# Gate stage of a hybrid decoder step: GpSimd takes key pages 0 and 2, VectorE 1 and 3, the sums run in another order, and the state's store is issued one piece sooner

## The reference, cut to what matters

```python
# attend_sample: q (8, 1, 8 heads, 2, 64), k_past (8, 512, 8, 2, 64) through the page table
s_past = einsum('bqhcd,bkhcd->bhcqk', q, k_past) * scale
p = softmax(s)[:, :, 0] - lam * softmax(s)[:, :, 1]
o = einsum('bhqk,bkhv->bqhv', p, v_past) + (the new token's own share)
# hgrn_steps, one step per sample
S = exp(g) * S + k * v
o = q . S
```

## Time and profile before

| what | us |
|---|---|
| median of 3 runs | 2257.0 |
| the three runs | 2255.3, 2257.0, 2257.14 |
| the profiled execution, its own time | 2256.59 |
| its span in the trace | 2254.8 |
| what lies around the span | 1.8 |
| gate stage on PE, first to last piece | 1092.7 to 1271.7 |
| PE busy over the span | 2221.8 (99%) |
| DVE, ACT, POOL busy over the span | 1542.2 (68%), 1140.3 (51%), 957.7 (42%) |

### The profile page before, as it was taken

How to read it: one execution, slowest core, us unless ns; L and a number is a source line. 1 busy time by engine, 2 the same in 40 slices (tenths; PEclk the granted TensorE clock), 3 DMA queues, 4 the chain that set the end, 5 groups by cost and what they waited for, 6 DMA issues and landing times. The chain is left out here.

```text
span 2254.8 us, 47757 instructions
## 1 busy us (share of the span) xinstructions
PE 2221.8 (99%) x18881; PEld 2104.7 (93%) x18881; DVE 1542.2 (68%) x2534; ACT 1140.3 (51%) x2343; POOL 957.7 (42%) x1149
## 2 busy tenths in 40 slices
PE   7999999999999999999999999999999999999999
PEld 5899998989999999989888899999999999999999
DVE  4668677777767687776678515417988888876535
ACT  6666665666666666665433402015466666643110
POOL 1135262634444352635444314442155666535431
PEclk9999999999999999999999999999999999999999
DMA  8212122231213121221699713111355554485212
GB/s 308 85 54 90 48 86 67 58 105 55 99 48 105 42 81 60 67 95 39 237 363 353 272 41 123 48 48 62 129 188 188 184 191 180 181 310 194 88 47 95
DMA packets 103513, 288.34 MB, mean 128 GB/s; under 512 B 18426, under 2 KB 26490, under 8 KB 103290
## 3 DMA queue, kind: packets, MB, share of 16 engines
q1 hardware_dynamic: 102138, 281.09, 35.7%
q10 hardware_dynamic: 1152, 4.19, 0.5%
HBM read 213.18 MB, written 63.77 MB: 123 GB/s over the span
## 5 line engine op out<-in xcount | busy, mean ns | idle before, releaser
L172 PE MATMUL h_G<-xn_hi,h_w_hi 128*128 128x344 f32 x1368 | 457.8, 335 | 0.2 <-ACT h_d_oraw L920 0.2
L172 PE MATMUL h_G<-xn_hi,h_w_lo 128*128 128x344 f32 x1368 | 437.3, 320 | 0.0
L172 PE MATMUL h_G<-xn_lo,h_w_hi 128*128 128x344 f32 x1368 | 437.0, 319 | 0.0
L1205 POOL TENSOR_TENSOR h_w_lo<-h_w_raw,h_w_hi 128x1024 fp32r<-128x1024 f32 x58 | 149.3, 2574 | 385.5 <-ACT h_w_hi L782 349.8
L172 PEld LDWEIGHTS h_G<-xn_hi,h_w_hi 128*128 128x128 f32 x1368 | 258.6, 189 | 32.6 <-issue 21.2
L172 PEld LDWEIGHTS h_G<-xn_lo,h_w_hi 128*128 128x128 f32 x1368 | 257.3, 188 | 4.6
L172 PEld LDWEIGHTS h_G<-xn_hi,h_w_lo 128*128 128x128 f32 x1368 | 257.3, 188 | 0.0
L3094 DVE SCALAR_TENSOR_TENSOR x<-t_ps,keep_mod,x 128x344 f32<-128x344 f32 x168 | 94.2, 570 | 161.9 <-PE t_ps L2931 99.5
L2931 PE MATMUL t_ps<-f_act_lo,f_d_hi 128*128 128x344 f32 x528 | 169.5, 321 | 0.0
L2931 PE MATMUL t_ps<-f_act_hi,f_d_lo 128*128 128x344 f32 x528 | 168.9, 320 | 0.0
L2931 PE MATMUL t_ps<-f_act_hi,f_d_hi 128*128 128x344 f32 x528 | 168.4, 319 | 0.0
(11 more groups left out here) (471 smaller groups left out, 6997.1 us busy)
## 6 DMA issues: line engine op xcount, KB each, us to landing
h_w_raw<-in_w_in SPq DMA_DIRECT2D x72, 512.0 KB, 3.7
y_rows<-f_y SPq DMA_DIRECT2D x44, 516.0 KB, 2.7
f_y_pair<-y_rows SPq DMA_DIRECT2D x22, 1032.0 KB, 5.2
h_d_ada_w<-in_w_ada SPq DMA_DIRECT2D x32, 512.0 KB, 4.2
g_kp<-in_cache_k SPq DMA_DIRECT2D x32, 512.0 KB, 6.3
g_vp<-in_cache_v SPq DMA_DIRECT2D x32, 512.0 KB, 5.8
f_a<-in_w_ffn SPq DMA_DIRECT2D x57, 256.0 KB, 2.7
h_w_raw<-in_w_mix SPq DMA_DIRECT2D x24, 512.0 KB, 3.6
```

The costliest lines, as they stand in the source:

```text
L172: ins = eng.matmul(out, w[:, k * P:(k + 1) * P], x[:, k, columns], start=(k == 0 and n == 0), stop=(k == n_k - 1 and n == 2))
L1205: pool.tensor_tensor(wlo[w][:, :], raw[r][:, :], whi[w][:, :].bitcast(F32), ALU.subtract).then_inc(lo_done.sem, 1)
```

## The change

GpSimd multiplies pages 0 and 2 in place of 2 and 3, VectorE 1 and 3 in place of 0 and 1. VectorE sums the pages in the order 1, 0, 3, 2, and SP's and POOL's waits count by that order: the load of the next sample's page j still waits for the sum of page j. ACT issues the state's store ahead of the evacuation of piece `TURN_AT[i] + 1`, one piece sooner; the `finish_tile` that went with the last store stays where it was. No operation is added or removed.

```diff
+SUM_ORDER = (1, 0, 3, 2)
+POOL_KEYS = (0, 2)
@@ sync
-                    sp.wait_ge(k_summed.sem, k_summed.at(i, j + 1))
+                    sp.wait_ge(k_summed.sem, k_summed.at(i, SUM_ORDER.index(j) + 1))
@@ scalar
-                if n - 2 in TURN_AT:
-                    i = TURN_AT.index(n - 2)
+                if n - 1 in TURN_AT:
+                    i = TURN_AT.index(n - 1)
                     act.wait_ge(st_new.sem, st_new.at(i, 1))
                     act.dma_start(flat(o["s_state"][bass.ds(i, 1)]), st[:, :]).then_inc(st_out.sem, 16)
-                    if i == NS - 1:
-                        for t in cut_tiles(i):
-                            finish_tile(t)
+                if n - 2 == TURN_AT[NS - 1]:
+                    for t in cut_tiles(NS - 1):
+                        finish_tile(t)
@@ gpsimd
-                for j in (2, 3):
+                for j in POOL_KEYS:
@@ vector
-                for j in range(PAGES):
-                    if j < 2:
+                for j in SUM_ORDER:
+                    if j not in POOL_KEYS:
...
-                        dve.wait_ge(k_scaled.sem, k_scaled.at(i, j - 1))
+                        dve.wait_ge(k_scaled.sem, k_scaled.at(i, POOL_KEYS.index(j) + 1))
```

## The result

| kernel | median, us | runs | lowest to highest |
|---|---|---|---|
| before | 2256.52 | 6 | 2255.30 to 2258.20 |
| changed | 2266.50 | 6 | 2263.12 to 2269.64 |

The changed kernel is slower: the ratio is 1.0043 (95% interval 1.0033 to 1.0053), 10.0 us in the medians. The profiled execution took 2268.26 us (span 2266.5), 11.7 more than the profiled one of before.

The account below looks back on a forecast made before the run. PE, busy 99% of the span, was taken as the bound; -0.3 + 0.75 + 2.4 + 2.8 - 0.9 - 0.4 + 0.5 = +4.9 us gave 2261.9 us, range 2253.5 to 2267.

Parts of the forecast that it names:

- the store's landing: Gate stage: store taken to land in 7.5 us, bounds 3.7 or no gain; first key page 19.7 us behind store issue.
- the steps for turns 0 to 6: Gate stage, between successive samples' score transposes: +0.75 first, +2.4 for the next three, then +2.8, -0.9 and -0.4 us.
- The lock: Gate stage: such DVE operations and POOL multiplications exclude each other for whole instructions; whichever asked first goes first.
- `low` behind POOL's pages: Gate stage: in some turns `low` asks ahead of DVE's page 3, costing between 0 and 2.4 us; +0.5 taken.
- turn 5: Sample 5's gate turn: next page 0 lands 9.7 us after its score transposes start, behind both cuts; -0.9 us.
- the rival in which the store lands fast: Gate stage: store needs 3.7 us, POOL's passes fall among the state update's multiplications; 2265.4 us, chance 0.15.
- Turn 4: Sample 4's gate turn: POOL's page 0 holds line 1972, PE waits 2.5 us for the state; 23.6 us long, +2.8.
- Turn 6: Sample 6's gate turn: the next page 0 comes behind `cut`, keys end at 17.9 where before 18.3; -0.4 us.
- T7: Start of sample 7's score transposes: PE still waits over 2 us there, clock loss kept, everything behind moves along.
- turn 0's own keys: Sample 0's keys at the gate stage's start: between 0 and 0.65 us of PE's wait goes; -0.3 taken.
- the store at the end of the state update: Gate stage: the store goes out when the new state is ready, 7.8 us after the score transposes start.
- nothing lost in ACT's queue: Gate stage: the store moves past one evacuation, one issue is 0.34 us; taken to cost nothing.

Follow-up runs that it names:

- pool_behind_cut: The changed kernel, with POOL's key multiplications held until DVE's `cut` of the turn is done: 2259.03 us, ratio 1.0010.
- order_only: The changed kernel's page order and shares, with the state's store back at its old place: 2264.23 us, ratio 1.0033.
- pool_memset: The changed kernel with each POOL key multiplication replaced by three memsets of the page, products of pages 0 and 2 left out: 2252.51 us, ratio 0.9980.

## Why the prediction was right, and where its sizes were off

The sign and the mechanism were right, and the time lay in the range, near its upper end. The sum was half of what came: +4.9 against +10.0. That the time still fell into the range is owed to the range's width, which was drawn for the bounds of the store's landing. In the sum itself a slip is without weight: 20.0 + 20.6 + 20.0 less 58.1 is 2.5 and not 2.4, which would make the total 4.95 in place of 4.85. With the last experiments each half can be weighed: POOL's pages ahead of DVE are worth 7.5 us (pool_behind_cut) where the steps for turns 0 to 6 sum to 4.65, and `low` is worth 4.2 where the step had 0.5. The two take away 11.7 one at a time and 12.1 together.

*The lock, and who goes next: right but for one row.* Turn 0 of the changed kernel, DVE, then POOL, beside the earlier trace rows:

```profile
1115.61 2.86 DVE L1895 TENSOR_SCALAR gate_a<-gate_a 128x1032 f32<-128x1032 f32 x1
1118.39 3.40 DVE L1905 TENSOR_TENSOR g_kp<-g_kp,gate_b 128x1024 f32<-128x1024 f32 x1
1121.83 2.34 DVE L1909 TENSOR_REDUCE g_s_tok<-g_kp 128x16 f32<-128x1024 f32 x2
1124.09 3.37 DVE L1905 TENSOR_TENSOR g_kp<-g_kp,gate_b 128x1024 f32<-128x1024 f32 x1
...
1115.51 5.20 POOL L1874 TENSOR_TENSOR g_kp<-g_kp,gate_b 128x1024 f32<-128x1024 f32 x2 [5.72 <-DMA g_kp<-in_cache_k]
1123.99 2.39 POOL L1868 TENSOR_TENSOR h_w_lo<-h_w_raw,h_w_hi 128x1024 fp32r<-128x1024 f32 x1 [3.28 <-ACT h_w_hi L1702]
```

POOL asks for page 0 at T + 7.7 (1115.51), 0.1 us ahead of `cut`, which waits and takes 2.86; DVE's page 1 ends at 1121.79, T + 14.0. Both are to the tenth what was forecast. Turn 1 (19.75 for 20.0) and turn 2 (20.4 for 20.6) came within 0.3, though turn 2 by another course, below.

*`low` behind POOL's pages: mis-sized.* The next row of DVE is where it fails. Page 3's multiplication is asked for at 1124.09, `low` at 1123.99, so it takes 3.37 in place of 1.2: 2.1 us in turn 0, which the step knew as a bound for all turns together and gave 0.5. The bound was that of one pass; the same happens in turn 3 too, there to page 1. In turn 6 of this kernel `low` came behind page 1 and was itself held; only in pool_behind_cut does it hold page 3 there. Before, both of DVE's multiplications stood at the head of the turn and only sums, which nothing held, were left by the time `low` came. In the order 1, 0, 3, 2 a multiplication stands late in the turn, and it meets `low`.

*The store's landing: mis-sized, with turns 2, 3, 5 and 6.* The step took 7.5 us, "since the same loads stand ahead of it". Stores 1 to 4 landed in 4.7, 4.5, 5.6 and 5.2, while stores 5 and 6 needed 8.3 and 8.1. SP's key loads and next state load, which follows the landing, and ACT's store of sample 1; first of the changed kernel, then of pool_behind_cut:

```profile
1128.79 3.66 SPq L1621 DMA_DIRECT2D g_kp<-in_cache_k  x4
1142.36 0.33 SPq L1624 DMA_DIRECT2D g_st<-in_state  x1
...
1137.62 0.34 ACTq L1741 DMA_DIRECT2D out_s_state<-g_st  x1
```

```profile
1128.75 3.66 SPq L1621 DMA_DIRECT2D g_kp<-in_cache_k  x4
1141.70 0.33 SPq L1624 DMA_DIRECT2D g_st<-in_state  x1
...
1134.59 0.34 ACTq L1741 DMA_DIRECT2D out_s_state<-g_st  x1
```

The key loads go out at the same time in both. The store goes 3.0 us later in the changed kernel, since its turn 0 was longer, and is down only 0.7 later: 9.9 us behind the end of the key loads' issue (1128.79 + 3.66) against 9.3. Stores 2 to 4, issued 3.8 to 4.5 later than in pool_behind_cut by the same measure, are down 1.3 to 1.8 later. So the loads ahead weigh more in the landing than the store's own issue, and in a stretched turn they have drained further. In order_only a store as late as T + 15.5 landed in 5.0. The key pages therefore came sooner against the stretched turns: from store to POOL's start on the next-but-one sample's page 0 it took 16.7 us in turn 2, 16.3 in turn 3 and 17.2 in turn 5, where the step had 19.7; 20.3 in turn 6. In turn 5 POOL began at T + 7.1, where 9.7 was forecast, and held both cuts (2.69 and 2.88). So the rival in which the store lands fast came half true: POOL's passes fell among the state update in turns 2 and 3, turns 5 and 6 took 21.1 and 19.9 where it gave 20.6 and 20.0 and the sum 19.2 and 17.9, and its 2265.4 is nearer to the result than the forecast. But no store landed in its 3.7 us, and those of turns 5 and 6 needed over 8. Of the page DMA: Bandwidth & Descriptors of the Trainium skill ("Queues, rings and completion order") it was said that by its rule of taking queues in turn the store would not stand behind SP's loads. The rows on store 1 lean against that, without settling it. That the draining is the cause is read from the rows of these kernels, not isolated by a run of its own.

What the sooner pages do, POOL above DVE, in turn 2 and turn 3:

```profile
1154.33 7.52 POOL L1874 TENSOR_TENSOR g_kp<-g_kp,gate_b 128x1024 f32<-128x1024 f32 x2 [1.02 <-DMA g_kp<-in_cache_k]
...
1153.93 1.20 DVE L1966 TENSOR_TENSOR g_st<-g_st,keep_s_f 128x1024 f32<-128x1024 f32 x1
1155.07 1.21 DVE L1972 TENSOR_TENSOR g_vB<-g_vB,keep_s_kk 128x1024 f32<-128x1024 f32 x1
1156.31 3.32 DVE L1974 TENSOR_TENSOR g_st<-g_st,g_vB 128x1024 f32<-128x1024 f32 x1
```

```profile
1175.95 6.16 POOL L1874 TENSOR_TENSOR g_kp<-g_kp,g_qB 128x1024 f32<-128x1024 f32 x2 [5.74 <-DMA g_kp<-in_cache_k]
...
1176.56 3.31 DVE L1974 TENSOR_TENSOR g_st<-g_st,g_vB 128x1024 f32<-128x1024 f32 x1
```

POOL asks at T + 4.7 and T + 5.9, so it is the state update, not `cut`, that is held first (3.3 for 1.2), and PE waits 0.9 and 0.7 for the weights that DVE copies next. Turn 3 then has `low` on top: 21.9. Turn 2 also holds the row that doesn't fit: POOL asked at 1154.33, within line 1966, yet line 1972, asked at 1155.07, went ahead of it and took its undisturbed 1.21; only line 1974 was held. So the one that asked first does not always go first. Why it did not here is open.

*Turn 4: right.* Its rows, DVE, then POOL, beside the earlier trace rows:

```profile
1200.57 1.50 DVE L1972 TENSOR_TENSOR g_vB<-g_vB,keep_s_kk 128x1024 f32<-128x1024 f32 x1
1202.10 3.26 DVE L1974 TENSOR_TENSOR g_st<-g_st,g_vB 128x1024 f32<-128x1024 f32 x1
1205.28 2.87 DVE L1895 TENSOR_SCALAR gate_b<-gate_b 128x1032 f32<-128x1032 f32 x1
...
1200.94 6.66 POOL L1874 TENSOR_TENSOR g_kp<-g_kp,gate_b 128x1024 f32<-128x1024 f32 x2
```

The state is ready at 1205.36, T + 13.4 (forecast 13.5), PE waits 2.26 for it (2.5), the turn lasts 23.5 (23.6). The second wait forecast, at T5, isn't there: PE lost 1.7 us to half speed behind the first wait (the window at 1205), and by the time it came to T5, DVE was done.

*Turn 6, decided by a hair.* Page 0 was put behind `cut`; POOL began at T + 7.66, 0.15 us ahead of `cut`. *T7* was said to move along at an unchanged cost; its wait grew to 4.27 us and the half-speed stretch with it, +0.9.

*Right too:* turn 0's own keys (-0.4 for -0.3), the store at the end of the state update (store 0 alone went out 1.0 us behind it), and nothing lost in ACT's queue: the waits of PE listed above all end with DVE.

## What to carry to other kernels

When work moves between two engines that exclude each other, the number of instructions says little: lay out who asks when, and put every instruction that can be held where the other engine can't arrive first, with those that can't be held (here the sums) behind it. A placement that hangs on a tenth of a microsecond is priced at its worst case for each turn in which it may happen, not once. A lost turn also moves everything timed by transfers, so a forecast made with the old arrival times should be run through a second time with the new ones.

## What the runs showed of the hardware

- Memsets on POOL don't hold DVE's multiplication of two tiles (1.21 us beside them), but they do hold `cut`, an operation on one tile: 1.00 in turn 0 above, ending 0.55 us behind the end of the first memset (1114.80 + 0.97), and the half-page memset, 0.53 undisturbed, took 0.96 across it. The page SBUF — State Buffer of the Trainium skill ("Who interferes with whom") separates the same two cases: an instruction of GpSimd that only writes doesn't contend with VectorE's two-input ones, while `tensor_scalar` can enter a mode that contends with GpSimd.
- A `cut` that waits can be passed. In turn 1 of pool_memset it asked at 1134.53, while `low` ran until 1136.67; POOL's memset, asked at 1136.60, went ahead of it, and `cut` ended 0.55 behind the memset. In the changed kernel `cut` went ahead of POOL's multiplication in the same place. POOL, then DVE, in pool_memset:

```profile
1133.35 3.32 POOL L1870 TENSOR_TENSOR h_w_lo<-h_w_raw,h_w_hi 128x1024 fp32r<-128x1024 f32 x1 [7.93 <-ACT h_w_hi L1702]
1136.60 0.95 POOL L1876 MEMSET g_kp<- 128x1024 f32 x1
...
1134.53 3.57 DVE L1901 TENSOR_SCALAR gate_b<-gate_b 128x1032 f32<-128x1032 f32 x1
```

- The half-speed stretch is not a matter of one wait's length alone: in one and the same execution the granted clock is 0.81 behind PE's wait of 2.26 us at 1205.41, 0.81 within the wait of 4.27 at T7 and 0.66 behind it, but 1.00 around the wait of 2.70 at T1 (the windows above).
